# Fifth tile of x squared and scaled behind the first low parts; the gates' upper rows of the first tokens multiplied once for both halves

## The chip, the cores and the metric

The kernel runs on one core of one Trainium2 chip. The metric is the device time of one execution in microseconds (us); a measurement is the median of some executions.

## The reference

One layer of a hybrid block on x of 1024 tokens by 1024 channels, all float32: an RMS norm of x, one wide projection, an mLSTM branch and a dilated-attention branch, their gated sum, an output projection and a second RMS norm. What the change touches is the norm at the entry and the eight gate columns `if_pre`:

```python
h = rmsnorm(x, pre_w)
proj = h @ w_in
... if_pre ... = jnp.split(proj, idx, axis=-1)     # 2 * M_HEADS = 8 columns
gates = if_pre + b_if
i_pre = gates[..., :M_HEADS]
log_f = jax.nn.log_sigmoid(gates[..., M_HEADS:])
```

## The kernel before

**Splitting.** Every matrix product is made from float32 parts: a high part (a copy rounded to float32r, made by ScalarE) and a low part (the original less the high part, made by VectorE or GpSimd). A product is then three matmuls a k tile: high by high, low by high, high by low.

**Seven products a pair.** h, transposed, has 1024 channels by 1024 tokens and is cut in quadrants: B11 (upper channels, first tokens), B21 (lower channels, first tokens), T1 (upper channels, second tokens, less B11), B22 (lower channels, second tokens), and three more sums T2, T3, T4. Two columns of weight tiles (a "pair") are multiplied by it with seven products of 12 matmuls (P1 to P7) in place of eight. `seq` lists the products of all pairs; the first nine are P1, P2, P6, P5 of pair 0, P1 of pair 1, P7 of pair 0, P2 of pair 1, P4 and P3 of pair 0, and the tenth is P6 of pair 1. P1 reads B11, P2 reads B21, P6 reads T2, P5 reads T1, P7 reads T3, P4 reads T4, P3 reads B22. Each needs the high and the low part of its weights: for the products 0 to 3 the low part is made by GpSimd (`low`, L1077), for 4, 6, 7, 5 and 8 by VectorE or GpSimd by a table (`low_dve`, L375).

**The entry.** Eight tiles of 128 tokens of x arrive (`x_in`). Tiles 0 to 4 are squared and summed on ScalarE (`square`, L1504), get epsilon added on VectorE (`mean_square`, L2039), the reciprocal root on GpSimd (`reciprocal_root`, L1087), and are scaled on VectorE (`scale`, L2074). Tiles 5 to 7 are squared on VectorE (`late_square`, L2033) and scaled by a diagonal matrix that GpSimd makes (`diagonal`, L1094). TensorE transposes tiles 0 to 3 into eight banks (L1373). From each bank ScalarE makes the high part (`first_high`, L1510), VectorE the low part (`first_low`, L2043), and ScalarE a plain copy b_sb that frees the bank (`first_copy`, L1515). Product 0 waits for the first such copy. Behind product 1 TensorE transposes tiles 4 to 7 (`second_half`, L1380), from which ScalarE and VectorE make B22, T1, T2, and from those T3 and T4 with their high and low parts. All engines take their work in the order in which it is written; for the first nine products that order is written out by hand.

**The gates.** `iw` holds the gate columns' high and low parts side by side, so that a gate product of a k tile is two matmuls (high and low part of h). `gate_tokens` (L1249) multiplies for the first 512 tokens (half 0) B11 and B21, 16 matmuls, ahead of product 2, and for the second 512 tokens (half 1) B11, T1 and B22, 24 matmuls, ahead of product 8: B11 + T1 is the upper channels' part there. ScalarE copies both results into `gate_row` (L1583), SyncE sends it through DRAM into `gates4`, and VectorE reads it (`rows`, L1836).

The written orders that the change edits are, on ScalarE, L1529 to L1563; on VectorE, L2078 to L2083; on GpSimd, L1103 to L1107.

Of the kernel before, what the change touches and what calls it, by code (L numbers as in the profile page):

```python
# [13 lines left out]
P = 128  # L14
# [131 lines left out]
def hybrid_kernel(nc, x, w_in, w_if, w_pm, w_pa, w_out, b_gate, conv_wt, conv_bt, pre_wt, m_wt, post_w,  # L146
# [197 lines left out]
    for s in range(NSTEP):  # L344
        for it in items[s]:
            what = it[0]
            if what == "if":
                fill(("if", it[1]), "act")
# [50 lines left out]
    with ctx:  # L399
# [182 lines left out]
        x2_in = [sem(f"x2_in{i}") for i in range(4)]  # L582
# [7 lines left out]
        pe_y = sem("pe_y")  # L590

        x_sq = sem("x_sq")
# [6 lines left out]
        ring_act = sem("ring_act")  # L599
        keep_act = sem("keep_act")  # L600
# [8 lines left out]
        ysq_done, mg_hi = sem("ysq_done"), sem("mg_hi")  # L609

        v_step = sem("v_step")
        x_ms, x_sq_late, x_scaled = sem("x_ms"), sem("x_sq_late"), sem("x_scaled")
# [13 lines left out]
        m_ms, m_fac = sem("m_ms"), sem("m_fac")  # L626
# [3 lines left out]
        y_ms, y_read, y_done = sem("y_ms"), sem("y_read"), sem("y_done")  # L630

        g_ready = sem("g_ready")
        x_rs, x_norm = sem("x_rs"), sem("x_norm")
        s12_done = sem("s12_done")
        lo_pool = sem("lo_pool")
        m_rs, y_rs = sem("m_rs"), sem("y_rs")
# [136 lines left out]
        def _(sp):  # L773
# [95 lines left out]
            def piece(it):  # L869
# [9 lines left out]
                elif what == "if_out":  # L879
                    ring_taken(sp, ("if", 1))  # L880
# [152 lines left out]
            def x_again(t):  # L1033
                if t < 4:
                    sp.wait_ge(mg_done, 13 + t)
                else:
                    sp.wait_ge(y_done, t - 3)
                sp.dma_start(gst[t % 4][:], x[t * P:(t + 1) * P, :]).then_inc(x2_in[t % 4], 16)
# [19 lines left out]
        def _(g):  # L1058
# [28 lines left out]
            def reciprocal_root(t):  # L1087
                if t < 5:
                    g.wait_ge(x_ms, t + 1)
                else:  # L1090
                    g.wait_ge(x_sq_late, t - 4)
                TT(ssq[:, NT + t:NT + t + 1], ssq[:, t:t + 1], halfneg[:, 0:1], ALU.pow).then_inc(x_rs, 1)

            def diagonal(t):  # L1094
                reciprocal_root(t)
                g.wait_ge(x_rs, t + 1)
# [23 lines left out]
            for k in range(NSTEP):  # L1120
# [5 lines left out]
                for it in pool_late[k]:  # L1126
                    what = it[0]
                    if what == "norm":
                        h = it[1]
                        g.wait_ge(m_ms, h + 1)  # L1130
                        TT(mrs[:], msq[:, h % 2], halfneg[:], ALU.pow).then_inc(m_rs, 1)
            for t in range(NT):
                g.wait_ge(y_ms, t + 1)
                TT(yrs[:, t:t + 1], ysum[:, t:t + 1], halfneg[:, 0:1], ALU.pow).then_inc(y_rs, 1)
# [3 lines left out]
        def _(pe):  # L1138
# [110 lines left out]
            def gate_tokens(half):  # L1249
                b = work(("if", half))  # L1250
                if half == 0:
                    pe.wait_ge(iw_lo_done, 1)
# [1058 lines left out]
```

## Time and profile before

| | us |
|---|---|
| median of 3 runs | 1369.98 (1368.76 to 1371.14) |
| the profiled execution | 1369.94 |
| its span in the trace | 1368.1 |
| TensorE busy with matmuls | 1352.3 (99%) |
| VectorE, ScalarE, GpSimd busy | 794.5, 641.7, 569.2 |
| share of the chain that ended last on TensorE | 91% |

The span runs from the first to the last instruction; 1.8 us of the execution's time lie around it. Busy shares are means over the whole span: the entry is one stage and the rest another, and they are read apart by stretches. A matmul's duration in the trace is longer than the distance to the next, since matmuls overlap: 128x512 ones last about 390 ns and follow each other every 228 ns.

### The profile page before, as it was taken

What the parts mean: (1) busy time and instruction counts of PE and PEld (TensorE: products, weight loads), DVE (VectorE), ACT (ScalarE), POOL (GpSimd) and SP (SyncE); (2) the same over time, 40 slices, a digit from 0 to 9 for tenths busy, and PEclk for the clock granted to TensorE, in tenths of its full rate; (3) what the DMA queues carried; (4) which work ended last, traced back from release to release, by engine and by line L of the source; (5) the groups of instructions that cost most, each with busy time, mean ns of one, the idle gap of its engine ahead of it and who ended that gap; (6) DMA issues with size and microseconds to landing.
All of it is one profiled execution on the core that took longest, in us unless ns stands there. A gap on an engine that the chain in (4) does not pass through costs nothing.

```text
span 1368.1 us, 18779 instructions
## 1 busy us (share of the span) xinstructions
PE 1352.3 (99%) x6470; PEld 1127.3 (82%) x6470; DVE 794.5 (58%) x1260; ACT 641.7 (47%) x1320; POOL 569.2 (42%) x400
## 2 busy tenths in 40 slices
PE   7999999999999999999999999999999999999998
PEld 5788888888888888888888888888888888888786
DVE  5874438346543835877756575755644442997632
ACT  6644543543444455345445445544544553533421
POOL 5253435335443534654434445344333544454000
PEclk9999999999999999999999999999999999999999
DMA  6132233324233323455442634345343354966421
GB/s 194 51 76 65 69 74 90 96 48 126 76 85 72 84 79 61 149 173 144 114 145 66 188 104 134 100 127 175 87 150 97 93 188 165 345 200 196 183 97 58
DMA packets 210462, 165.02 MB, mean 121 GB/s; under 512 B 32400, under 2 KB 186544, under 8 KB 210368
## 3 DMA queue, kind: packets, MB, share of 16 engines
q1 hardware_dynamic: 210224, 163.75, 40.5%
q8 instruction: 53, 0.87, 0.3%
q14 instruction: 41, 0.34, 0.1%
q10 hardware_dynamic: 144, 0.07, 0.0%
HBM read 117.41 MB, written 40.08 MB: 115 GB/s over the span
## 4 chain that ended last, share of the span: by engine, by line
PE 91%; DVE 4%; issue 2%; ACT 1%; DMA 1%; SPq 1%; POOL 0%; DVEq 0%; POOLq 0%; ACTq 0%
PE proj L1244 69%; PE side L1189 3%; PE proj L1189 2%; PE side L1289 2%; PE side L1268 2%; PE side L1345 2%; PE side L1354 2%; PE proj L1170 2%; PE side L1170 2%; PE side L1277 1%; PE side L1317 1%; PE side L1350 1%; PE side L1300 1%; DMA x_sb<-x_in 1%; PE side L1362 1%
## 5 line engine op out<-in xcount | busy, mean ns | idle before, releaser
L1080 POOL TENSOR_TENSOR w_lo<-raw,w_hi 128x512 fp32r<-128x512 f32 x161 | 234.5, 1458 | 413.8 <-ACT w_hi L1456 413.7
L1244 PE MATMUL proj<-hi_T,w_hi 128*128 128x512 f32 x832 | 338.1, 406 | 2.2 <-ACT snap L1474 1.6
L1244 PE MATMUL proj<-hi_T,w_lo 128*128 128x512 f32 x832 | 325.2, 391 | 0.0
L1244 PE MATMUL proj<-lo_T,w_hi 128*128 128x512 f32 x832 | 324.1, 390 | 0.0
L1244 PE MATMUL proj<-hi_B,w_hi 128*128 128x512 f32 x624 | 254.1, 407 | 5.6 <-ACT b_sb L1518 4.0
L1244 PE MATMUL proj<-hi_B,w_lo 128*128 128x512 f32 x624 | 244.2, 391 | 0.0
L1244 PE MATMUL proj<-lo_B,w_hi 128*128 128x512 f32 x624 | 243.6, 390 | 0.0
L1080 POOL TENSOR_TENSOR w_lo<-s_sb,w_hi 128x512 fp32r<-128x512 f32 x104 | 156.7, 1510 | 153.5 <-ACT w_hi L1456 153.4
L1244 PEld LDWEIGHTS proj<-hi_T,w_hi 128*128 128x128 f32 x832 | 156.4, 188 | 36.0 <-issue 3.5
L1244 PEld LDWEIGHTS proj<-hi_T,w_lo 128*128 128x128 f32 x832 | 156.1, 188 | 34.2
L1244 PEld LDWEIGHTS proj<-lo_T,w_hi 128*128 128x128 f32 x832 | 156.6, 188 | 30.4
L1456 ACT ACTIVATE w_hi<-raw 128x512 fp32r<-128x512 f32 x216 | 135.2, 627 | 70.5 <-PE proj L1244 57.6
L1244 PEld LDWEIGHTS proj<-hi_B,w_hi 128*128 128x128 f32 x624 | 117.7, 189 | 29.9 <-ACT b_sb L1518 4.2
L1244 PEld LDWEIGHTS proj<-hi_B,w_lo 128*128 128x128 f32 x624 | 117.4, 188 | 25.4
L1244 PEld LDWEIGHTS proj<-lo_B,w_hi 128*128 128x128 f32 x624 | 117.8, 189 | 22.8
L1074 POOL TENSOR_TENSOR s_sb<-s_sb,raw 128x512 f32<-128x512 f32 x52 | 82.9, 1594 | 91.3 <-DVE w_lo L1887 90.5
L1456 ACT ACTIVATE w_hi<-s_sb 128x512 fp32r<-128x512 f32 x156 | 97.7, 627 | 37.9 <-PE proj L1244 28.9
L1887 DVE TENSOR_TENSOR w_lo<-s_sb,w_hi 128x512 fp32r<-128x512 f32 x52 | 43.9, 845 | 85.5 <-ACT w_hi L1456 85.5
L1068 POOL TENSOR_TENSOR s_sb<-raw 128x512 f32<-128x512 f32 x52 | 75.5, 1453 | 21.5 <-DVE w_lo L1887 21.4
L2001 DVE SCALAR_TENSOR_TENSOR tmp<-stage,cw,tmp 128x1023 f32<-128x1023 f32 (+2 forms) x48 | 76.1, 1585 | 0.7
L2144 DVE CUSTOM_DVE_ANT_0 prob<-side,mask_sb 128x128 f32<-128x128 f32 (+1 forms) x96 | 29.2, 347 | 67.3 <-PE side L1268 67.2
L1474 ACT ACTIVATE snap<-proj 128x512 f32<-128x512 f32 x52 | 31.1, 597 | 78.0 <-PE proj L1244 77.9
(253 smaller groups left out, 2014.5 us busy)
## 6 DMA issues: line engine op xcount, KB each, us to landing
raw<-w_in SPq DMA_DIRECT2D x95, 512.0 KB, 6.0
m_spill<-stage SPq DMA_DIRECT2D x16, 1024.0 KB, 5.6
chunk<-m_spill SPq DMA_DIRECT2D x32, 512.0 KB, 3.8
gate_spill<-stage SPq DMA_DIRECT2D x8, 1024.0 KB, 4.3
gst<-gate_spill SPq DMA_DIRECT2D x32, 256.0 KB, 3.2
share<-share_spill SPq DMA_DIRECT2D x12, 512.0 KB, 5.0
x_sb<-x_in SPq DMA_DIRECT2D x8, 512.0 KB, 7.6
hm_spill<-stage SPq DMA_DIRECT2D x4, 1024.0 KB, 8.8
```

What stands on the lines that cost most here:

```text
L1068: ins = TT(s1_sb[:], a21, a22, ALU.add)
L1074: ins = TT(s2_sb[:], s1_sb[:], a11, ALU.subtract)
L1080: TT(w_lo_ring[k % RING][:], src, w_hi_ring[k % RING][:].bitcast(F32), ALU.subtract).then_inc(lo_pool, 1)
L1170: mm = pe.matmul(pa_slot(t)[:, tokens], w[:, kt, :], m[:, kt, tokens], start=(kt == 0 and w is wh and m is at_hi), stop=(kt == AH - 1 and ...
L1189: mm = pe.matmul(y_slot(t)[:, columns], a[:, kt, :], w[i][:, j, columns], start=(kt == 0 and a is hi_part and w is out_hi), stop=(kt == KT ...
L1244: mm = pe.matmul(acc(p, which), w[:, kt, :], m[:, kt, :], start=(first and kt == 0 and w is wh and m is h_hi[b]), stop=(kt == 3 and w is w ...
L1268: mm = pe.matmul(b[:, at_ * P:(at_ + m) * P], qo_sb[(NG * h + g) % 4][:, n * P:(n + 1) * P], k_sb[g][:, (n + 1 - m) * P:(n + 1) * P], star ...
L1456: A(w_hi_ring[k % RING][:], src, ACT.Copy).then_inc(hi_done, 1)
L1474: A(snap[0][:], a, ACT.Copy).then_inc(u3_done, 1)
L1887: TT(w_lo_ring[k % RING][:], operand(p, weight_name(k)), w_hi_ring[k % RING][:].bitcast(F32), ALU.subtract).then_inc(lo_dve, 1)
L2001: ins = STT(t_[:, d:], src[:, 0:S - d], cw[:, t, 3 - d:4 - d], t_[:, d:], ALU.mult, ALU.add)
L2144: ins = V.tensor_tensor_reduce(out=prob_part(h, i)[:, part], in0=b[:, part], in1=mask, scale=-ASCALE, scalar=3.0e38, op0=ALU.add, op1=ALU. ...
```

## The change

1. **Order of the fifth tile.** On ScalarE `square(4)` moves from behind `high(0)` to behind `first_high(1)`. On VectorE `mean_square(4)` and `scale(4)` leave the loop ahead of the first low parts: `mean_square(4)` comes behind `first_low(2)`, `scale(4)` behind `late_square(5)`. On GpSimd `reciprocal_root(4)` comes behind `low(0)` in place of ahead of it.
2. **Gates.** A new step `if_top` ahead of product 2 multiplies B11 alone (8 matmuls) into the bank. ScalarE copies that partial sum into the second half of `gate_row`, between the high part T2,3 and the high part T1,0. The B21 part of half 0 (8 matmuls) moves to ahead of product 4, accumulates onto the same bank, and waits for that copy. Half 1 is then T1 and B22 alone, 16 matmuls, and VectorE adds its result to the stored part in place of ScalarE's copy. SyncE's `if_out` waits for both halves.
3. **Semaphores.** Several are merged with offsets (`row_sq`, `mean_sq`, `root`, `x_in` for the second reading of x); no instruction is added or moved by it.

```diff
-    items[2].append(("if", 0))
+    items[2].append(("if_top",))
+    items[4].append(("if", 0))
     items[8].append(("if", 1))
-    act_late[2].append(("if", 0))
-    act_late[8].append(("if", 1))
+    act_late[4].append(("if", 0))
+    dve_late[9].append(("if", 1))
...
                 elif what == "if_out":
+                    ring_taken(sp, ("if", 0))
                     ring_taken(sp, ("if", 1))
...
             for t in range(4):
                 reciprocal_root(t)
+            low(0)
             reciprocal_root(4)
-            low(0)
             low(1)
...
+            def gate_top_rows():
+                copied(pe, 2)
+                pe.wait_ge(iw_lo_done, 1)
+                gate_tokens(bank[0], [(kt, "B11") for kt in range(4)], True, False).then_inc(pe_gate, 1)
+
+            def gate_half(half):
+                b = work(("if", half))
+                if half == 0:
+                    pe.wait_ge(gate_top, 1)
+                    mm = gate_tokens(b, [(kt, "B21") for kt in range(4, 8)], False, True)
+                else:
+                    mm = gate_tokens(b, [(kt, name) for name, o in (("T1", 0), ("B22", 4)) for kt in range(o, o + 4)],
+                                     True, True)
                 mm.then_inc(pe_ring, 1)
...
             high(0)
-            square(4)
             act.wait_ge(start_in, 16 * NSTART)
             first_high(0)
             first_high(1)
+            square(4)
             first_copy(0)
...
             h_high("T2", 3, 8)
+            act.wait_ge(pe_gate, 1)
+            A(gate_row[:, half_of(1)], bank[0], ACT.Copy).then_inc(gate_top, 1)
             for j in range(4):
                 h_high("T1", j, 2 * j + 1)
...
+                elif what == "if":
+                    dve.wait_ge(pe_ring, ring_no["if", 1] + 1)
+                    dve.wait_ge(gate_top, 1)
+                    TT(gate_row[:, half_of(1)], bank[ring_no["if", 1] % BANKS], gate_row[:, half_of(1)], ALU.add
+                       ).then_inc(ring_dve, 1)
...
-            for t in range(5):
+            for t in range(4):
                 mean_square(t)
                 scale(t)
-            for kt in range(4):
+            for kt in range(3):
                 first_low(kt)
+            mean_square(4)
+            first_low(3)
             late_square(5)
+            scale(4)
             first_low(4)
```

## Rows read from the trace of the kernel before

**Rows 1.** Stretches: us, busy (count) of PE, PEld, DVE, ACT, POOL; clock; DMA.

```profile
17.20:20.00 2.80, 2.77 (x7) 2.19 (x8) 2.21 (x3) 2.80 (x6) 0.00 (x0) 0.50 1.20 290
20.00:26.60 6.60, 4.97 (x19) 3.10 (x18) 5.70 (x10) 5.10 (x10) 6.28 (x6) 0.99 0.22 50
36.80:55.00 18.20, 17.70 (x74) 13.06 (x73) 17.82 (x30) 12.74 (x24) 0.00 (x0) 1.00 0.07 18
63.50:1368.10 1304.60, 1296.52 (x6211) 1085.13 (x6209) 748.06 (x1188) 600.59 (x1248) 544.84 (x372) 1.00 0.41 120
```

**Rows 2.** TensorE's waits over the whole run: total us, times, longest.

```profile
PE proj L1244 <- ACT b_sb L1518: 4.0, 1, 4.0
PE proj L1244 <- DVE lo_B L2046: 1.6, 2, 0.8
```

**Rows 3.** Chain that ended last, in order of time: start us, us, what.

```profile
36.90 2.18 ACT hi_T L1526 x4
...
43.83 0.69 DVE lo_T L2071
...
55.12 5.47 PE side L1259 x24
```

**Rows 4.** Timeline of ScalarE: start us, us, engine, line, operation, [idle before].

```profile
10.57 0.63 ACT L1456 ACTIVATE w_hi<-raw 128x512 fp32r<-128x512 f32 x1 [0.64 <-DMA raw<-w_in]
12.05 1.06 ACT L1508 ACTIVATE tmp<-x_sb 128x1024 f32<-128x1024 f32 x1 [0.85 <-DMA x_sb<-x_in]
...
13.11 1.25 ACT L1513 ACTIVATE hi_B<-proj,prew 128x512 fp32r<-128x512 f32 x2
16.49 0.69 ACT L1518 ACTIVATE b_sb<-proj,prew 128x512 f32<-128x512 f32 x1 [2.13 <-DVE lo_B L2046]
...
55.28 0.58 ACT L1583 ACTIVATE gate_row<-side 128x512 f32<-128x512 f32 x1
```

**Rows 5.** Timeline of VectorE, 11 to 23 us.

```profile
11.35 0.75 DVE L2076 TENSOR_SCALAR x_sb<-x_sb,ssq 128x1024 f32<-128x1024 f32 x1 [0.66 <-POOL ssq L1092]
...
14.05 1.74 DVE L2076 TENSOR_SCALAR x_sb<-x_sb,ssq 128x1024 f32<-128x1024 f32 x1 [0.66 <-POOL ssq L1092]
...
19.11 1.22 DVE L2036 CUSTOM_DVE_ANT_0 x_junk<-x_sb 128x1024 f32<-128x1024 f32 x1
...
20.92 1.65 DVE L2036 CUSTOM_DVE_ANT_0 x_junk<-x_sb 128x1024 f32<-128x1024 f32 x1
```

**Rows 6.** Timeline of GpSimd, 10 to 22 us.

```profile
10.77 0.55 POOL L1092 TENSOR_TENSOR ssq<-ssq,halfneg 128x1 f32<-128x1 f32 x1 [0.93 <-DVE ssq L2041]
...
13.99 1.26 POOL L1080 TENSOR_TENSOR w_lo<-raw,w_hi 128x512 fp32r<-128x512 f32 x1
20.08 1.41 POOL L1080 TENSOR_TENSOR w_lo<-raw,w_hi 128x512 fp32r<-128x512 f32 x1 [4.84 <-ACT w_hi L1456]
```

**Rows 7.** Timeline of TensorE, 17 to 64 us.

```profile
17.23 0.80 PE L1244 MATMUL proj<-hi_B,w_hi 128*128 128x512 f32 x1 [3.98 <-ACT b_sb L1518]
...
26.60 0.27 PE L1394 MATMUL proj<-ident,x_sb 128*128 128x128 f32 x1
...
63.51 0.48 PE L1244 MATMUL proj<-hi_T,w_hi 128*128 128x512 f32 x1
```

**Rows 8.** Timeline of VectorE, 57 us.

```profile
57.03 0.69 DVE L1887 TENSOR_TENSOR w_lo<-s_sb,w_hi 128x512 fp32r<-128x512 f32 x1
```

**Rows 9.** Timeline of GpSimd, 57 to 64 us.

```profile
57.86 1.30 POOL L1068 TENSOR_TENSOR s_sb<-raw 128x512 f32<-128x512 f32 x1 [21.37 <-DVE w_lo L1887]
...
61.34 2.54 POOL L1080 TENSOR_TENSOR w_lo<-s_sb,w_hi 128x512 fp32r<-128x512 f32 x2 [0.74 <-ACT w_hi L1456]
```

**Rows 10.** Timeline of SyncE's DMA issues, 66 us.

```profile
66.86 0.35 SPq L885 DMA_DIRECT2D gates<-if_spill  x1
```

**Rows 11.** DMA issues, 60 to 76 us: count, KB each, us to landing.

```profile
gates<-if_spill SPq DMA_DIRECT2D x1, 64.0 KB, 1.9
```

**Rows 12.** Timeline of VectorE, 75 us.

```profile
75.44 0.19 DVE L1841 TENSOR_REDUCE m_rows<-ident 32x8 f32<-32x32 f32 x1
```

More of the change, by code:

```diff
@@ L599, in hybrid_kernel @@
         ring_act = sem("ring_act")
+        gate_top = sem("gate_top")
         keep_act = sem("keep_act")
@@ L1247, in product, with gate_tokens @@
                 mm.then_inc(pe_prod, 1)
[L1249 to L1252, printed above, removed]
-                    parts = [(kt, name) for name, o in (("B11", 0), ("B21", 4)) for kt in range(o, o + 4)]
-                else:
-                    parts = [(kt, name) for name, o in (("B11", 0), ("T1", 0), ("B22", 4)) for kt in range(o, o + 4)]
+            def gate_tokens(b, parts, first, last):
                 for i, (kt, name) in enumerate(parts):
@@ L1258, in gate_tokens @@
                     for m in (h_hi[name], h_lo[name]):
-                        mm = pe.matmul(b[:], iw[:, kt, :], m[:, kt % 4, :], start=(i == 0 and m is h_hi[name]),
-                                       stop=(i == len(parts) - 1 and m is h_lo[name]))
+                        mm = pe.matmul(b, iw[:, kt, :], m[:, kt % 4, :], start=(first and i == 0 and m is h_hi[name]),
+                                       stop=(last and i == len(parts) - 1 and m is h_lo[name]), skip_group_check=True)
+                return mm
+            def gate_top_rows():
[10 more added lines that the diff above has]
+                                     True, True)
                 mm.then_inc(pe_ring, 1)
@@ L1401, in _ @@
                     what = it[0]
-                    if what == "if":
-                        gate_tokens(it[1])
+                    if what == "if_top":
+                        gate_top_rows()
+                    elif what == "if":
+                        gate_half(it[1])
                     elif what == "cols":
@@ L1580, in piece @@
                 if what == "if":
-                    half = it[1]
-                    act.wait_ge(pe_ring, ring_no["if", half] + 1)
-                    A(gate_row[:, half * HALF:(half + 1) * HALF], bank[ring_no["if", half] % BANKS][:], ACT.Copy
-                      ).then_inc(ring_act, 1)
+                    act.wait_ge(pe_ring, ring_no["if", 0] + 1)
+                    A(gate_row[:, half_of(0)], bank[ring_no["if", 0] % BANKS], ACT.Copy).then_inc(ring_act, 1)
                 elif what == "log":
@@ L2020, in piece @@
                         dve.wait_ge(sq_done, NT * (h + 1))
-                        TS(msq[:, h % 2], msq[:, h % 2], 1.0 / MD, 4.0 * EPS, ALU.mult, ALU.add).then_inc(m_ms, 1)
+                        TS(msq[:, h % 2], msq[:, h % 2], 1.0 / MD, 4.0 * EPS, ALU.mult, ALU.add).then_inc(mean_sq, 1)
                     else:
-                        dve.wait_ge(m_rs, h + 1)
+                        dve.wait_ge(root, ROOT_M + h + 1)
                         TT(mfac[:], mrs[:], rden[:, h % 2], ALU.mult).then_inc(m_fac, 1)
+                elif what == "if":
+                    dve.wait_ge(pe_ring, ring_no["if", 1] + 1)
+                    dve.wait_ge(gate_top, 1)
+                    TT(gate_row[:, half_of(1)], bank[ring_no["if", 1] % BANKS], gate_row[:, half_of(1)], ALU.add
+                       ).then_inc(ring_dve, 1)
                 elif what == "small":
@@ L2231, in result @@
                     columns = half_of(half)
-                    dve.wait_ge(ysq_done, 2 * t + half + 1)
+                    dve.wait_ge(row_sq, SQ_Y + 2 * t + half + 1)
                     if half:
-                        STT(ysum[:, t:t + 1], ysq[:, t, 0:1], EPS, ysq[:, t, 1:2], ALU.add, ALU.add).then_inc(y_ms, 1)
+                        STT(ysum[:, t:t + 1], ysq[:, t, 0:1], EPS, ysq[:, t, 1:2], ALU.add, ALU.add).then_inc(mean_sq, 1)
                     elif t == 0:
@@ L2241, in result @@
                 dve.wait_ge(y_read, 2 * t + 2)
-                dve.wait_ge(y_rs, t + 1)
-                dve.wait_ge(x2_in[t % 4], 16 * (t // 4 + 1))
+                dve.wait_ge(root, ROOT_Y + t + 1)
+                dve.wait_ge(x_in[t], 32)
                 parts = [slice(0, DM)] if t < NT - 1 else [half_of(0), half_of(1)]
```

48 lines of the change are left out of this document (24 added, 24 removed).

## The prediction

> **What bounds the kernel now.** I read the stretches first [rows 1]. From 63.5 us to the end TensorE is busy for 1296.5 of 1304.6 us, at full clock. Whatever the change gains or loses must happen ahead of that point, and then it moves the end one for one, because nothing behind 63.5 us has slack to take it up or to give. The change edits only steps ahead of 66 us. In that part TensorE has idle time, and the list of its waits says for whom: 4.0 us once for the first plain copy b_sb, 1.6 us in two pieces for low parts of B21 [rows 2]. Then I read the chain that ended last [rows 3]: between 36.9 and 43.8 us it does not run on TensorE but through ScalarE's high parts into VectorE's low parts, and VectorE is busy 17.82 of 18.20 us from 36.8 to 55 us [rows 1]. So the entry is a chain of VectorE and ScalarE, with TensorE bound by itself only between 26.6 us and some 30 us and from 55 us on. The question for every part of the change is therefore: does it sit on that chain, and which engine is late at 63.5 us, when product 9 (P6 of pair 1) starts [rows 7]?
>
> **Part 1: eight gate matmuls less.** Half 1 had 24 gate matmuls in 5.47 us [rows 3], 0.228 us each; 16 are left, so 8 x 0.228 = 1.82 us of TensorE's time go. Half 0 keeps its 16, but 8 of them move from ahead of product 2 to ahead of product 4, where TensorE would otherwise wait: the chain of high and low parts sets when the products 2 to 7 can run, so this move neither costs nor gains (the cover is VectorE's 17.82 of 18.20 us [rows 1]; were it gone, the eight would still be the same eight). The 1.82 us lie at 58.6 to 60.4 us, in a stretch bound by TensorE. How much is kept depends on what is late next. Product 9 needs its weights' low part, and that comes along another chain: VectorE's low part of product 8 starts at 57.03 us and takes 0.69 us [rows 8]; it frees the buffer for GpSimd's first sum of pair 1, which starts at 57.86 us, and behind the second sum and ScalarE's high part GpSimd makes two low parts from 61.34 us in 2.54 us [rows 9], so the first is there at 61.34 + 1.27 = 62.61 us. Product 9 started at 63.51 us [rows 7]. It can come forward to about 62.65 us and no further while that chain stays where it is: **0.85 us of the 1.82 are kept, 0.97 are lost in a new wait** for GpSimd's low part.
>
> **Part 2: the added copy on ScalarE.** The copy of the partial gate sum is a 128x512 copy like the existing gate_row copy, 0.58 us [rows 4]; back to back such operations follow each other at less than their duration (four high parts in 2.18 us [rows 3], 0.54 each), so I take 0.5 us. It stands ahead of the high part T1,0, which is where the chain runs at 36.90 us [rows 3]. Its own input is early: the 8 matmuls behind the transposes end about 2 us before. Queued behind it on ScalarE are T1's and B22's high parts, two weight high parts, one snapshot and the first high part of T3, for which VectorE's low part at 43.83 us waits [rows 3]. There is no gap on ScalarE between, so that low part starts 0.5 us later, and with it VectorE's whole row of work to 57.03 us [rows 8] and the chain of part 1. **Cost 0.5 us on the chain** (0.3 if small gaps of VectorE take up some, 0.6 if the full duration counts). Half 1's copy, taken off ScalarE at 62.7 us, gains nothing there. Its substitute, an add on VectorE of about 0.7 us (as the low part in [rows 8]), comes behind VectorE's work at 65.6 us, where VectorE has nothing for some 5 us: nothing. It makes the gates ready for SyncE some 3 us later. Their way back was issued at 66.86 us [rows 10] and landed 1.9 us after its issue [rows 11]; VectorE reads them at 75.44 us [rows 12]. 66.86 + 3.1 + 0.35 + 1.9 = 72.2 us, 3 us early: nothing. SyncE's next queued issues, pair 3's weights, wait anyway for low parts of pair 1 at 71 us.
>
> **Part 3: the fifth tile moved.** In before, ScalarE squares tile 4 at 12.05 us, the first high part starts at 13.11 us and the first plain copy, for which product 0 waits, at 16.49 us [rows 4]; that copy waited for VectorE's first low part, which stood behind scale(4), from 14.05 us for 1.74 us [rows 5]. Taking scale(4) out of the way looks like 1.5 us. Two things take it back. **First, a collision.** The same scaling of tile 3 took 0.75 us [rows 5]; the scaling of tile 4 took 1.74 because GpSimd's low(0) had begun 0.06 us earlier, at 13.99 us for 1.26 us [rows 6]. The new order on GpSimd puts low(0) directly behind the root of tile 3, which starts at 10.77 us and takes 0.55 [rows 6], to 11.3 us; low(0)'s input, ScalarE's high(0), runs from 10.57 us for 0.63 us [rows 4] and is ready at 11.2 us. So low(0) starts at about 11.29 us, 0.06 us ahead of scale(3) at 11.35 us [rows 5]: the very pattern of tile 4 now falls on tile 3, which holds up the last transposes by 1.74 - 0.75 = 0.99 us. The first high part comes at about 13.45 us, the second at 14.0, the square of tile 4 at 14.6 to 15.7, the first copy at 15.7 in place of 16.49 us: product 0 starts 0.8 us earlier than 17.23 us [rows 7]. **Second, the work is only deferred.** scale(4) (0.75 us) and its epsilon (0.15 us) now lie between the low parts for which product 1 waits one by one. VectorE's row up to there gains 0.8 us and takes 0.9 us more. And scale(4) comes due as late_square(5) ends (1.22 us long [rows 5]), at which point GpSimd's low(1), held up by it, is due too, as at 20.08 us when it took 1.41 us [rows 6]. If low(1) goes first, scale(4) waits some 1.2 us, against which late_square(6), which took 1.65 us [rows 5] with low(1) beside it, gets 0.45 us shorter and a second wait of GpSimd's falls away; my walk through the three engines gives the low parts of B21 0.6 us late. If scale(4) goes first they are on time. I take the middle: **the transposes of the second tokens, at 26.60 us [rows 7], start 0.3 us later (0.0 to 0.6)**, and the chain behind them moves with them.
>
> The port is where a rule of the Trainium skill bears on this. It says ("SBUF — State Buffer", section "Who interferes with whom") that VectorE in a two-port mode and GpSimd share one pair of ports, that whoever issues first holds it for a whole instruction and that the other is fully blocked. The rows of tiles 3 and 4 above agree: 0.75 us alone, 1.74 us begun 0.06 us behind GpSimd. By that rule the order of two starts 0.06 us apart decides a whole microsecond, which is the rival "no collision" below.
>
> **The sum.** Front +0.3, copy +0.5, matmuls -0.85: -0.05 us. The span was 1368.1 us and 1.84 us lie around it, 1369.94 us for the profiled execution, 0.04 us from the median. 1369.94 - 0.05 = 1369.9 us.
>
> **The rivals.**
> - *No collision at tile 3.* If the first weights land only 0.1 us later, high(0) ends behind 11.35 us and scale(3) goes first. The last transposes then stay in place, product 0 starts about 1.7 us earlier, and with the deferred 0.9 us and the second collision the transposes at 26.60 us start 0.3 us earlier, 0.9 us if scale(4) also wins. -0.6 + 0.5 - 0.85 = -0.95: 1369.0 us. For it: margins of 0.06 us against the landing of a DMA. Against it: the profiled execution's own times.
> - *The cap is not there.* If the low part of product 9 is made early enough after all, or the copy finds a gap, all 1.82 us are kept: +0.3 + 0.5 - 1.82 = -1.0 us, or without a collision -1.9: 1368.0 to 1368.9 us. Against it stands the order GpSimd, ScalarE, GpSimd between 57.86 and 61.34 us [rows 9], which nothing in the change touches.
> - *Slower: TensorE's clock falls in product 1.* The granted clock was 0.50 (1.2 GHz) from 17.2 to 20 us, behind 3.98 us of idle time [rows 7], and 0.99 from 20 to 26.6 us [rows 1], with two idle pieces of 1.6 us together [rows 2]. The change starts product 0 earlier and product 1 no earlier, so TensorE's idle pieces before each k tile of B21 grow to 1.1 to 1.2 us. If the clock falls to the lower level there, the transposes from 26.60 us, 6.4 us of work bound by TensorE, run at half speed for, say, the 2.8 us of the low stretch of [rows 1]: +1.4 us, 1371.3 us; for all 6.4 us and a little of the gate matmuls, +3.2 to +6: 1373 to 1376 us. It decides as soon as the idle pieces ahead of the transposes bring the clock down, which those of 0.8 us did not and that of 3.98 us did.
> - *The gates come late.* Were the way through DRAM more than 3 us slower than I think, VectorE would stand still at 75 us and hold low parts: +0.5 to +1 us, 1370.7 us.
> - *The order does not matter at all* (the b_sb wait is taken by another input, such as the channel weights): the front term is +0.9 to 1.0, 1370.5 us; the change then does not do what its first part says.
>
> **How the numbers follow.** Forecast 0.45, no collision 0.25, no cap 0.1, clock 0.08 (half of it over 2.74 us), late gates 0.05, no effect of order 0.07. A difference of 0.2%, 2.74 us, is about what a measurement of this kernel can tell from no change. Only the high end of the clock case passes it upward: slower 0.04. Downward it takes no collision, no cap and both small races won (-2.8 us): faster 0.04. The rest, 0.92, is within. The cases without the clock lie between 1368.0 and 1370.9 us; the runs of before scatter by 1.2 us around their median, so a median of few moves by half of that: 1367.7 to 1371.4 us.
>
> **What would show it.** In the profile of after: scale(3) at 1.74 us with low(0) just ahead of it (or 0.75 us, the rival); the first b_sb copy at about 15.7 us; the first transpose of the second tokens at 26.9 us; the gate copy between two high parts near 37 us with no gap, and T3's first low part near 44.6 us; 16 gate matmuls ahead of product 8; a wait of some 0.9 us of TensorE ahead of product 9 or of pair 0's transposes of v, ended by GpSimd or ScalarE; product 9 at 63.5 us within 0.5. The prediction is wrong if product 9 starts by more than 1 us off that, if VectorE has gaps ahead of T3's low parts that take the copy up, or if the time behind product 9 is not 1304.6 us within its scatter.

## The result, and the profile after

| | before | after |
|---|---|---|
| median, us (20 runs each) | 1370.68 (1368.76 to 1372.31) | 1372.16 (1370.30 to 1375.04) |
| ratio after / before | | 1.0014 (95%: 1.0007 to 1.0020) |
| the profiled execution, us | 1369.94 | 1372.18 |
| its span | 1368.1 | 1370.4 |
| first transpose of the second tokens | 26.60 | 27.95 |
| product 9 starts | 63.51 | 64.25 |
| product 10 starts | 66.71 | 68.34 |
| product 10 to the end of the span | 1301.4 | 1302.0 |

The change costs 1 to 2.7 us. That is within 0.2% of before, as the largest of the chances had it, but 0.8 us above the upper end of the range. The stretches of after come first; the columns are those of [rows 1].

```profile
17.20:20.00 2.80, 2.80 (x9) 2.12 (x8) 2.80 (x6) 2.80 (x6) 1.20 (x2) 0.50 1.19 290
20.00:26.60 6.60, 4.52 (x12) 2.63 (x11) 6.27 (x9) 3.92 (x7) 6.30 (x7) 0.76 0.20 48
36.80:55.00 18.20, 17.03 (x73) 12.89 (x72) 17.41 (x29) 13.25 (x24) 0.78 (x1) 1.00 0.01 2
63.50:1370.40 1306.90, 1297.28 (x6212) 1085.39 (x6212) 747.81 (x1189) 601.49 (x1250) 547.13 (x373) 1.00 0.41 120
```

The granted clock from 20 to 26.6 us is 0.76 of full speed, where it was 0.99 [rows 1], and 12 matmuls ran there where 19 did. TensorE's waits of after (total us, times, longest):

```profile
PE proj L1251 <- ACT b_sb L1536: 2.3, 1, 2.3
PE proj L1251 <- DVE lo_B L2069: 2.1, 3, 1.1
...
PE side L1316 <- issue: 0.9, 1, 0.9
...
PE proj L1251 <- DVE k L1837: 0.6, 1, 0.6
```

The wait for b_sb is down from 4.0 to 2.3 us, that for low parts of B21 is up from 1.6 to 2.1 in three pieces [rows 2]. The last two rows are new. One, ahead of the transposes of v (L1316) and so of product 9, is the cap that the prediction had. The view names no releaser for it ("issue"); the copy vr_sb that these transposes read, made by ScalarE behind the two high parts that wait for GpSimd's second sum, ends 0.10 us ahead of them (63.18 + 0.58 = 63.76 us), and GpSimd's low part for product 9 ends at 64.1 us. The other, for VectorE's sum k (L1837) ahead of product 10, is not in the prediction at all.

VectorE and GpSimd at tiles 3 and 4, timeline (start us, us, engine, line, operation, [idle before <- what ended it]):

```profile
11.31 1.77 DVE L2099 TENSOR_SCALAR x_sb<-x_sb,ssq 128x1024 f32<-128x1024 f32 x1 [0.66 <-POOL ssq L1099]
...
19.58 1.76 DVE L2099 TENSOR_SCALAR x_sb<-x_sb,ssq 128x1024 f32<-128x1024 f32 x1
```

```profile
11.27 1.27 POOL L1087 TENSOR_TENSOR w_lo<-raw,w_hi 128x512 fp32r<-128x512 f32 x1
...
19.36 1.44 POOL L1087 TENSOR_TENSOR w_lo<-raw,w_hi 128x512 fp32r<-128x512 f32 x1 [0.86 <-ACT w_hi L1474]
```

GpSimd's low(0) begins 0.04 us ahead of scale(3), which takes 1.77 us where it took 0.75 [rows 5]; low(1) begins 0.22 us ahead of scale(4), which takes 1.76. TensorE in product 1 and up to the second tokens, and ScalarE with the added copy:

```profile
16.50 0.50 PE L1251 MATMUL proj<-hi_B,w_hi 128*128 128x512 f32 x1 [2.27 <-ACT b_sb L1536]
...
23.86 0.71 PE L1251 MATMUL proj<-hi_B,w_hi 128*128 128x512 f32 x1 [0.78 <-DVE lo_B L2069]
24.37 0.63 PE L1251 MATMUL proj<-lo_B,w_hi 128*128 128x512 f32 x1
24.80 0.63 PE L1251 MATMUL proj<-hi_B,w_lo 128*128 128x512 f32 x1
...
27.95 0.27 PE L1410 MATMUL proj<-ident,x_sb 128*128 128x128 f32 x1
```

```profile
15.76 0.69 ACT L1536 ACTIVATE b_sb<-proj,prew 128x512 f32<-128x512 f32 x1
...
37.99 0.58 ACT L1580 ACTIVATE gate_row<-side 128x512 f32<-128x512 f32 x1
38.47 1.66 ACT L1544 ACTIVATE hi_T<-sum_T 128x512 fp32r<-128x512 f32 x3
```

The matmuls from 24.37 us follow each other every 0.43 us: the lower of TensorE's two levels (1.2 GHz), for a second time. And this is the meeting that the prediction missed: two operations of VectorE and GpSimd that want the shared port at the same time. VectorE's and then GpSimd's timeline, with TensorE behind them:

```profile
64.14 1.76 DVE L1899 TENSOR_TENSOR s_sb<-raw,s_sb 128x512 f32<-128x512 f32 x1 [1.50 <-POOL w_lo L1087]
65.82 1.77 DVE L1905 TENSOR_TENSOR w_lo<-raw,w_hi 128x512 fp32r<-128x512 f32 x1
67.52 0.68 DVE L1837 TENSOR_TENSOR k<-snap,proj 128x512 f32<-128x512 f32 x1
68.11 0.68 DVE L2046 TENSOR_TENSOR gate_row<-side,gate_row 128x512 f32<-128x512 f32 x1
```

```profile
62.84 2.51 POOL L1087 TENSOR_TENSOR w_lo<-s_sb,w_hi 128x512 fp32r<-128x512 f32 x2 [0.74 <-ACT w_hi L1474]
65.72 1.32 POOL L1087 TENSOR_TENSOR w_lo<-raw,w_hi 128x512 fp32r<-128x512 f32 x1 [0.37 <-ACT w_hi L1474]
```

```profile
63.86 0.63 PE L1316 MATMUL side<-ident,vr_sb 128*128 128x128 f32 x4 [0.85 <-issue]
64.25 0.47 PE L1251 MATMUL proj<-hi_T,w_hi 128*128 128x512 f32 x1
...
68.34 0.47 PE L1251 MATMUL proj<-hi_T,w_hi 128*128 128x512 f32 x1 [0.64 <-DVE k L1837]
```

VectorE's low part of product 11, at 65.82 us, takes 1.77 us, because GpSimd's low part of product 12 began 0.10 us ahead of it. In before the same two came in the other order:

```profile
64.35 0.68 DVE L1887 TENSOR_TENSOR w_lo<-raw,w_hi 128x512 fp32r<-128x512 f32 x1
...
64.99 1.29 POOL L1080 TENSOR_TENSOR w_lo<-raw,w_hi 128x512 fp32r<-128x512 f32 x1 [1.12 <-ACT w_hi L1456]
```

k stands behind that low part on VectorE, so it comes 1.1 us later, and product 10 waits for it. The chain that ended last of after, in order of time, runs past product 9 through these very operations:

```profile
62.84 1.28 POOL w_lo L1087
...
64.14 0.21 DVE s_sb L1899
...
65.82 1.77 DVE w_lo L1905
67.59 0.61 DVE k L1837
...
68.34 3.68 PE proj L1251 x15
```

### The profile page after: what moved, and what is told of

It reads as the page before. It is cut to its first block, busy times and chain, and to the rows that moved or that the text cites. A ratio compares the mean times of both kernels' runs of the same rounds, so it can differ in the third digit from the quotient of the medians.

```text
span 1370.4 us, 18767 instructions
## 1 busy us (share of the span) xinstructions
PE 1352.3 (99%) x6462; PEld 1126.7 (82%) x6462; DVE 793.0 (58%) x1261; ACT 641.6 (47%) x1320; POOL 570.1 (42%) x400
## 4 chain that ended last, share of the span: by engine, by line
PE 86%; DVE 4%; issue 2%; DMA 2%; SPq 1%; ACT 0%; POOL 0%; DVEq 0%; POOLq 0%; ACTq 0%
PE proj L1251 65%; PE side L1196 3%; PE proj L1196 2%; PE side L1305 2%; PE side L1284 2%; PE side L1361 2%; PE side L1370 2%; PE proj L1177 2%; PE side L1177 2%; PE side L1293 1%; PE side L1333 1%; PE side L1366 1%; SPq L914 1%; PE side L1316 1%; DMA share<-share_spill 1%
```

## The experiments

All milestones are from timelines, one profiled execution of each kernel, in us. "T2" is the first transpose of the second tokens, and "copy's stretch" the distance from T2's first low part to T3's first low part (both on VectorE), in which the added copy lies. "T3 to product 9" starts at T3's first low part. It is the cleanest measure of what an edit behind the copy does: T2 to T2's first low part takes about 9.4 us in some kernels and about 9.65 in others (9.54 in e10, 10.74 in e3) for reasons that lie ahead of the gates' half, and "T2 to product 9" carries that difference with it.

| kernel | T2 | copy's stretch | T2 to product 9 | T3 to product 9 | product 9 to 10 | VectorE low part of product 11 | product 10 |
|---|---|---|---|---|---|---|---|
| before | 26.60 | 7.59 | 36.91 | 19.68 | 3.20 | 0.68 | 66.71 |
| after | 27.95 | 7.99 | 36.30 | 18.92 | 4.09 | 1.77 | 68.34 |
| e1_order_alone | 27.46 | 7.59 | 36.62 | 19.65 | 3.21 | 0.68 | 67.29 |
| e2_gates_alone | 26.76 | 8.00 | 36.55 | 18.90 | 4.10 | 1.77 | 67.41 |
| e3_low0_behind | 28.18 | 7.99 | 37.64 | 18.91 | 4.10 | 1.77 | 69.92 |
| e5_gates_copy_in_gap | 27.84 | 7.59 | 36.87 | 19.63 | 4.09 | 1.77 | 68.80 |
| e8_low12_behind_low11 | 26.53 | 7.99 | 36.27 | 18.90 | 3.20 | 0.68 | 66.00 |
| e9_gates_low12_behind | 25.63 | 7.99 | 36.54 | 18.90 | 3.19 | 0.68 | 65.36 |
| e10_no_collision | 27.38 | 8.00 | 36.45 | 18.91 | 3.19 | 0.68 | 67.02 |
| e11_filled_gaps | 27.88 | 8.00 | 36.30 | 18.91 | 4.09 | 1.78 | 68.27 |
| e13_gates_low12_low8 | 27.41 | 8.00 | 36.02 | 18.63 | 3.19 | 0.68 | 66.62 |
| e14_copy_gap_low12 | 26.26 | 7.59 | 36.64 | 19.67 | 3.20 | 0.68 | 66.10 |
| e12_copy_gap_low8_low12 | 28.07 | 7.59 | 36.87 | 19.64 | 3.21 | 0.68 | 68.15 |
| e7_before_low8_first | 25.75 | 7.60 | 36.88 | 19.65 | 3.20 | 0.68 | 65.83 |

The front needs columns of its own, since two DMA landings move it. In the old order T2 hangs on the landing of the fifth tile of x: it comes 12.55 us behind the start of scale(4) in e9 (13.08 to 25.63 us) and in e12 (15.52 to 28.07 us), 2.4 us apart. So 26.60 us of before is one draw. In the six kernels with the new order, ScalarE squares the fifth tile at 14.1 to 15.0 us without a wait, so this landing did not set T2 in them; that of the start weights did in two (e3, e11):

| kernel | scale(3): start, us | to first b_sb | b_sb to T2 | both | clock 20 to 26.6 us |
|---|---|---|---|---|---|
| before (old order) | 11.35, 0.75 | 5.14 | 10.11 | 15.25 | 0.99 |
| after | 11.31, 1.77 | 4.45 | 12.19 | 16.64 | 0.76 |
| e1_order_alone | 11.62, 1.75 | 4.42 | 11.42 | 15.84 | 0.99 |
| e3_low0_behind | 11.20, 0.75 | 4.34 | 12.64 | 16.98 | 0.76 |
| e8_low12_behind_low11 | 11.69, 0.75 | 3.43 | 11.41 | 14.84 | 1.00 |
| e10_no_collision | 11.70, 0.75 | 3.43 | 12.25 | 15.68 | 0.57 |
| e11_filled_gaps | 11.33, 0.75 | 4.17 | 12.38 | 16.55 | 1.00 |

The intervals of the ratios below reach some 1.2 us to either side, so of 1 us and less the traces tell more than the medians.

### Each half of the change alone

e1 is the kernel before with the new order of the fifth tile, no gate edit:

```diff
+            low(0)
             reciprocal_root(4)
-            low(0)
...
             first_high(1)
+            square(4)
...
+            mean_square(4)
+            first_low(3)
             late_square(5)
+            scale(4)
```

> The kernel before with the fifth tile's new order alone; the gates stay as they were. Theory (the new order is the loss, through three costs on one chain: the scaling of tile 3 held up by GpSimd's low(0), the scaling of tile 4 by low(1), and TensorE's clock lower ahead of the second transposes): the first transpose of the second tokens starts about 27.9 us in place of 26.60, GpSimd's first sum of pair 1 about 1.1 us later than 57.86, and since nothing shortens TensorE's work the kernel is 1.1 to 2.0 us slower than before. Rival (the gates' new copy and the split are the loss, the order is even): within 0.3 us of before, product 9 at 63.5 us.

Measured: median 1371.21 us, ratio 1.0002 (0.9993 to 1.0011). scale(3) took 1.75 us beside low(0), and T2 came 15.84 us behind its start, 0.59 us more than in before. TensorE waited 1.12, 0.78 and 0.84 us ahead of three k tiles of product 1, and yet the clock stayed up:

```profile
20.00:26.60 6.60, 3.85 (x15) 2.22 (x13) 6.57 (x9) 3.90 (x7) 6.30 (x7) 0.99 0.22 48
```

So at T2 the order alone, with the collision and with the clock kept, is worth the upper end of what was forecast for it (0.6 us). Some of it comes back at once: in before GpSimd's last diagonal matrix was ready only at 27.26 us, behind T2 (26.60), and TensorE's first group of six transposes by it took 0.93 us from start to start of the next group; with the new order the matrix is ready ahead of T2 and the group takes 0.67 us. Counted from scale(3), T2's first low part is 0.33 us later than in before (25.22 and 24.89 us), and product 10 is 0.31 us later (55.67 and 55.36 us). In the time that is not told from nothing. The 1.1 us and more of the expectation were missed.

e2 is the opposite, the gates' half alone:

```diff
+            reciprocal_root(4)
             low(0)
-            reciprocal_root(4)
...
-            for t in range(4):
+            for t in range(5):
                 mean_square(t)
                 scale(t)
```

> The change without the fifth tile's new order: gates multiplied once, the copy of the partial sum ahead of T1's high parts. Theory (the order is the loss; the gates' part costs 0.4 us of chain for the copy and keeps 0.8 us of the 1.82): T3's first low part at 44.2 us, product 9 at 63.1 us, 0.4 us faster than before. Rival (the gates' part is the loss): slower than before by 0.5 us or more.

Measured: median 1371.33 us, ratio 1.0006 (0.9997 to 1.0015). Up to product 9 it went as expected: T3's first low part 0.40 us later against T2's, product 9 at 63.31 us, 36.55 us behind T2 in place of 36.91. These 0.36 us are +0.40 for the copy and -0.76 for the eight matmuls. But product 10 started 4.10 us behind product 9, not 3.20. VectorE's and GpSimd's timelines of e2:

```profile
64.89 1.77 DVE L1905 TENSOR_TENSOR w_lo<-raw,w_hi 128x512 fp32r<-128x512 f32 x1
66.59 0.67 DVE L1837 TENSOR_TENSOR k<-snap,proj 128x512 f32<-128x512 f32 x1
```

```profile
64.79 1.33 POOL L1087 TENSOR_TENSOR w_lo<-raw,w_hi 128x512 fp32r<-128x512 f32 x1 [0.37 <-ACT w_hi L1474]
```

The same meeting as in after, with the same margin of 0.10 us. It belongs to the gates' half: all five kernels that have that half and leave this order alone show it (after, e2, e3, e5, e11), with margins of 0.10 us, and e1 does not. From T2 to product 10 e2 needs 40.65 us and before 40.11: the gates' half, meant to save 1.8 us of matmuls, loses 0.5.

### The meeting at 65 us taken away

Theory from here on: the gate edit lets TensorE, and with it ScalarE, come forward against VectorE's chain. ScalarE no longer has the gate copy (62.68 us in before) and the transposes of v, whose copy it makes next, come earlier, so it hands product 12's high part to GpSimd before VectorE gets to product 11's low part. That these two causes bring ScalarE forward is read from the timelines; no run parts them. Rival: the wait for k is a matter of VectorE's lateness alone, and would be there without GpSimd. The edit holds GpSimd back by one operation; e8 is after with it, e9 is e2 with it:

```diff
+                    if k == 9:
+                        low_wait(g, 11)
                     low(k + LEAD)
```

> The changed kernel with one wait more: GpSimd's low part of product 12 waits until VectorE has made the low part of product 11. Theory (in the changed kernel these two meet, since TensorE and ScalarE come forward against VectorE; GpSimd wins by 0.1 us and VectorE's low part takes 1.77 us in place of 0.68, which holds up the sum that product 10 waits for): VectorE's low part of product 11 takes 0.7 us, TensorE's wait of 0.6 us ahead of product 10 goes, product 10 starts 3.2 us behind product 9 in place of 4.1, and the kernel is 0.9 us faster than the changed one. Rival (that wait only takes the place of one that comes anyway): product 10 moves by less than 0.3 us and the time stays.

> The gates' part alone with the same wait more, the fifth tile as in the kernel before. Theory: product 9 at 63.3 us and product 10 at 66.5 us, both 0.2 us ahead of the kernel before, which gives 0.2 us less than before; against the gates' part alone (product 10 at 67.4 us) 0.9 us less. Rival (the gates' part loses by something else): product 10 stays at 67.4 us or the gain is lost behind it.

Measured: e8 1370.75 us, 1.0001 (0.9993 to 1.0010); e9 1369.76 us, 0.9994 (0.9986 to 1.0003), where the change itself stands at 1.0014. VectorE and GpSimd in e9:

```profile
63.75 0.68 DVE L1907 TENSOR_TENSOR w_lo<-raw,w_hi 128x512 fp32r<-128x512 f32 x1
64.35 0.68 DVE L1839 TENSOR_TENSOR k<-snap,proj 128x512 f32<-128x512 f32 x1
```

```profile
64.50 1.29 POOL L1087 TENSOR_TENSOR w_lo<-raw,w_hi 128x512 fp32r<-128x512 f32 x1 [1.23 <-DVE w_lo L1907]
```

The low part takes 0.68 us again, in both kernels, and product 10 follows product 9 by 3.20 and 3.19 us. T2 to product 10 is 39.73 us in e9, against 40.65 in e2 and 40.11 in before. That is the 0.9 us of the missed step, and the rival is out. By the medians the step is only suggested: the interval of e8 touches that of after. With the meeting gone the gates' half does what was forecast for it: 0.38 us earlier than before. In e8 low(0) also happened to come at 11.79 us, 0.10 us behind scale(3), which took 0.75 us while low(0) took 1.78 us. From scale(3) to T2 it needed 14.84 us, 1.00 less than e1 with the collision and the same clock, and 0.41 less than before: the rival "no collision at tile 3", which had 0.3.

### The collisions at the front taken away

e3 is after with low(0) held behind scale(3):

```diff
+            g.wait_ge(x_scaled, 4)
             low(0)
```

> The changed kernel with one wait more: GpSimd's low(0) waits until tile 3 is scaled. Theory (the first collision is real but mostly hidden: product 1 waits for low parts that stand behind late squares and the deferred scaling, not for product 0): scaling of tile 3 takes 0.75 us in place of 1.77, the last transposes start at 12.1 us, the first copy b_sb at 14.8 us, the low parts of B21 come 0.3 to 0.9 us earlier, and the kernel gains 0.3 to 1.2 us on the changed one. Rival (the collision has no share in the loss): no difference from the changed kernel, 1.5 us over before.

Measured: 1372.32 us, 1.0012 (1.0004 to 1.0021), no better than after. scale(3) took 0.75 us, but two things ate the microsecond. ScalarE's first high part, timeline of e3, now waited for the start weights:

```profile
13.34 1.26 ACT L1532 ACTIVATE hi_B<-proj,prew 128x512 fp32r<-128x512 f32 x2 [1.16 <-DMA ifw<-w_if]
```

so b_sb came 4.34 us behind scale(3), not 3.43 as in e8. And the clock was low again from product 1's later k tiles on and into the transposes behind T2: 12.64 us from b_sb to T2, and T2's first low part 10.74 us behind T2 instead of 9.39. The expectation was missed by a landing and by the clock, not by the port of tile 3. (The collision of scale(4) with low(1) was still there, 1.77 us.) e10 holds both low(0) and low(1) behind their scalings, and has the edit of e8:

```diff
+            g.wait_ge(x_scaled, 4)
             low(0)
             reciprocal_root(4)
+            g.wait_ge(x_scaled, 5)
             low(1)
```

> The changed kernel with three waits more on GpSimd: low(0) behind the scaling of tile 3, low(1) behind that of tile 4, the low part of product 12 behind that of product 11. Theory (three meetings on the shared ports plus the low clock are the loss): both scalings and the low part take 0.75, 0.75 and 0.68 us, the low parts of B21 come 1.0 us earlier than in the changed kernel, product 10 starts at 66.3 to 66.8 us, and the kernel is 1.5 to 2.2 us faster than the changed one, no slower than before. Rival (the new order is worse by itself): product 10 behind 67.5 us.

Measured: 1370.03 us, 0.9995 (0.9986 to 1.0003), 2.1 us less than after by the medians. Both scalings took 0.75 us; late_square(6) now met low(1), 1.85 us in place of 1.21, and TensorE waited 2.2 us for that low part. The last low part of B21 came at 24.52 us, 1.0 us earlier than in after, as expected; product 10 came at 67.02 us, a little later than the 66.3 to 66.8 of the expectation. By the ratios to before, e10 (0.9995) and after (1.0014) are clear of each other. The clock, e3's windows row above e10's:

```profile
20.00:26.60 6.60, 4.16 (x12) 2.08 (x11) 6.06 (x9) 3.90 (x7) 6.30 (x8) 0.76 0.30 77
```

```profile
20.00:26.60 6.60, 5.21 (x11) 3.22 (x12) 5.26 (x8) 4.18 (x9) 6.30 (x7) 0.57 0.22 51
```

From b_sb to T2 the two kernels with the clock kept need 11.41 and 11.42 us (e8, e1), the three with the fallen clock 12.19 to 12.64 (after, e10, e3). So the collision at tile 3 is worth 1.0 us where no landing covers it (e1 against e8), and the fallen clock costs 0.8 us in after and in e3 1.2 us up to T2 and 1.35 us behind it (10.74 for 9.39). In e3 it stayed low until 31.0 us, in after until 27.4 us. e10 is another case: its clock was 1.00 up to 20.9 us, through all of product 0, fell in the wait of 2.2 us for low(1), and stayed low until 27.7 us, so its 0.84 us has more than one cause.

e11 fills TensorE's idle pieces in product 1 of after with small matmuls, whose results are overwritten:

```diff
+                        if name == "P2" and kt < 3:
+                            copied(pe, 3)
+                            for i in range((4, 6, 6)[kt]):
+                                pe.matmul(pb[2][:, 0:P], ident[:], ident[:], start=True, stop=True)
```

> The changed kernel with 16 matmuls of 128 columns more, which fill TensorE's idle pieces in product 1 (4, 6 and 6 ahead of its first three k tiles) and whose results are overwritten. Theory (the granted clock falls a second time because those pieces are long): the granted clock stays at its upper level from 20 to 27 us, the k tiles of product 1 take 0.7 us each in place of 1.3, the transposes of the second tokens start 0.7 us earlier than in the changed kernel, 27.2 us, and the kernel is 0.5 to 0.7 us faster than the changed one. Rival (the fall comes from something else): the clock falls there all the same and the time stays.

Measured: 1371.71 us, 1.0009 (1.0000 to 1.0017). The clock was 1.00 from 20 to 26.6 us, but each six of the small matmuls took 1.26 us, more than the pieces that they were to fill, and T2 came at 27.88 us. Since e8's clock also stayed up with the pieces unfilled, the run says nothing on what keeps it.

### The copy in another place

e5 is e2 with the copy between T3's second and third high parts, where ScalarE waits for sums, and the B21 matmuls ahead of product 5 instead of 4:

```diff
-    items[4].append(("if", 0))
+    items[5].append(("if", 0))
...
             for j in range(2):
                 h_high("T3", j, 9 + j)
+            act.wait_ge(pe_gate, 1)
+            A(gate_row[:, half_of(1)], bank[0], ACT.Copy).then_inc(gate_top, 1)
             for j in range(2, 4):
```

> The gates' part alone in another order: the copy of the partial sum stands between T3's second and third high part, where ScalarE had a gap of 0.76 us, and the B21 half is multiplied ahead of pair 0's P7. The fifth tile is as in the kernel before. Theory (the copy costs by where it stands): T3's first low part stays at 43.8 us, product 9 comes at 62.7 us, 0.8 us faster than before and 0.4 us faster than the gates' part with the copy ahead of T1. Rival (the copy's place is free): the same as the gates' part alone.

Measured: 1372.46 us, 1.0009 (1.0000 to 1.0018). T3's row is 7.59 us, as in before: the copy's 0.40 us are gone. But T2 to product 9 is 36.87 us, 0.32 more than in e2, so 0.7 us are lost behind T3. ScalarE and VectorE in e5:

```profile
51.05 0.60 ACT L1492 ACTIVATE snap<-proj 128x512 f32<-128x512 f32 x1 [2.28 <-PE proj L1251]
```

```profile
52.20 0.69 DVE L2096 TENSOR_TENSOR lo_T<-sum_T,hi_T 128x512 fp32r<-128x512 f32 x1 [0.82 <-ACT hi_T L1544]
```

The eight matmuls, moved to ahead of product 5, put that product and its snapshot back. ScalarE stands still 2.28 us for it (1.42 in e2), with T4's high parts queued behind, and VectorE 0.82 us, where it had no such gap in e2. From T3's first low part to product 9 e5 needs 19.63 us, as before does, where e2 needs 18.90. So the place ahead of product 4 was free and the next one is not. e14 is e5 with the edit of e8:

> The gates' part with the copy of the partial sum between T3's second and third high part, the B21 half ahead of P7 of pair 0, and the low part of product 12 behind that of product 11. Theory (the copy costs 0.4 us by its place): from VectorE's first low part of T2 to its first of T3 7.6 us as in the kernel before, in place of 8.0; 0.4 us faster than the same with the copy ahead of T1 (e9). Rival: no difference.

Measured: 1370.44 us, 1.0004 (0.9995 to 1.0013). T2 to product 9 is 36.64 us against 36.54 in e9: no gain over leaving the copy on the chain. The 0.40 us of the copy are gained (7.59 for 7.99) and 0.77 us lost behind it (19.67 for 18.90).

### The cap ahead of product 9

GpSimd's first sum waits for VectorE's low part of product 8 [rows 8, 9]. That low part was moved ahead of B22's last two low parts:

```diff
-            for j in range(4):
+            for j in range(2):
                 h_low("B22", j, 8 + j + 1, h_ready["B22"])
...
+            for j in range(2, 4):
+                h_low("B22", j, 8 + j + 1, h_ready["B22"])
```

e13 is e9 with it, e7 is before with it, and e12 is e5 with it and the edit of e8.

> The gates' part alone, low part of product 12 behind that of product 11, and VectorE's low part of product 8 two places earlier (behind the second of B22's four low parts in place of the fourth). Theory (the prediction's cap: of the 1.82 us one microsecond is lost because product 9 waits for GpSimd, whose chain starts at that low part): GpSimd's first sum of pair 1 comes 1.2 us earlier against the first copy b_sb, product 9 comes 1.0 us earlier against it, the kernel is about 1 us faster than the same one without this edit (e9). Rival (the cap is VectorE's own row, or ScalarE's snapshot): product 9 moves by less than 0.4 us.

> The kernel before with one edit: the low part of product 8 two places earlier. Theory (in the kernel before TensorE itself is the bound between its 24 gate matmuls and product 9, so GpSimd's chain has 0.9 us of slack there): GpSimd's first sum 1.2 us earlier, product 9 where it was, time within 0.2 us. Rival (the chain was the bound already before): faster by 0.5 us or more.

> All three edits: copy in the gap, low part of product 8 two places earlier, low part of product 12 behind that of product 11; the fifth tile as in the kernel before. Theory: the 1.82 us of the eight matmuls are kept whole, about 1.8 us (0.13%) faster than the kernel before, the fastest of all. Rival (a new meeting of GpSimd and VectorE or another wait ahead of product 10 takes the gain back): less than 0.8 us.

Measured: e13 1370.42 us, 0.9997 (0.9988 to 1.0006); e7 1370.22 us, 0.9999 (0.9990 to 1.0008); e12 1370.74 us, 0.9999 (0.9990 to 1.0008). In e7 the cap is not what binds: T2 to product 9 is 36.88 us against 36.91, as it should be where TensorE itself is late. In e13 it is 36.02 us against 36.54 in e9, but 0.25 of these 0.52 us lie between T2 and T2's first low part (9.39 and 9.65 us), far ahead of the edit. From T3's first low part to product 9 it is 18.63 against 18.90 us: 0.27 us gained where 1.0 was expected, and so the case of the rival (less than 0.4). GpSimd's timeline of e13:

```profile
57.64 2.21 POOL L1075 TENSOR_TENSOR s_sb<-raw 128x512 f32<-128x512 f32 x1 [20.58 <-DVE w_lo L1907]
```

Against T3's first low part the sum came 1.20 us earlier than in e9 (12.84 and 14.04 us), as expected, but took 2.21 us where it takes 1.30 [rows 9]: it now stands beside VectorE's last two low parts of B22, of which the first began ahead of it. The chain moved ahead ran into the same port from the other side. In e7 the sum took 1.60 us and VectorE's two low parts 2.38, where two take 1.29. e12 gained nothing of the copy's 0.4 us: 36.87 us to product 9, with VectorE's two low parts at 2.39 us. The expected 1.8 us did not come; the rival's case did.

## Why the prediction was wrong, by its steps

The sum of the profiled executions is closed: T2 +1.35, T2's first low part -0.25 against T2, copy +0.40, matmuls -0.76 (what is left of product 9's +0.74), product 9 to 10 +0.89, behind product 10 +0.61; together 2.24 us, the difference of the two executions. Against the forecast of -0.05 us the miss is 2.3 us: 0.9 at product 10, 0.8 at the front (1.10 for 0.3), 0.6 behind product 10, and the two other terms even out.

- **What bounds the kernel: right up to its last step.** Ahead of 63.5 us it is the chain through ScalarE and VectorE. But "nothing behind 63.5 us has slack", taken to mean that product 9 carries the result, was the step that failed. The change moves VectorE's low part of product 11 by +1.47 us and GpSimd's low part of product 12, which follows ScalarE and TensorE, by +0.73. The trace of before had the margin: the first began 0.64 us ahead of the second (64.35 and 64.99 us). A relative shift of 0.74 us turned that into 0.10 us behind. The working followed the chain to product 9 and stopped there; its sentence that the gate copy taken off ScalarE "gains nothing there" looked at the copy's own time and not at what ScalarE then hands on earlier. **+0.89 us, missed whole**; e2 shows it with the gates' half alone, e8 and e9 take it away.
- **Matmuls: right.** -0.85 us forecast of 1.82, -0.76 measured (19.68 to 18.92 us); the cap by GpSimd's chain is there, as a wait of 0.85 us ahead of the transposes of v. The rival without the cap is out; e13, by an edit of its own, won 0.27 us of it.
- **The copy: right.** +0.5 us forecast, +0.40 to 0.41 measured in all eight kernels with the copy ahead of T1's high parts, and 0 where the copy was moved (e5, e14, e12). VectorE had no gap to take it up.
- **The front: right in kind, mis-sized.** +0.3 us (0.0 to 0.6) forecast, +1.35 measured at T2 and +1.10 at T2's first low part, from where the chain goes on. VectorE's part, the last low part of B21 at 25.54 us in place of 24.97, is +0.57 at T2 and, with the 0.25 us that come back behind T2, +0.32 on the chain: e1, with 0.59 and then 0.33, shows the same, and that is the forecast. scale(3) at 1.77 us and b_sb at 15.76 us came as forecast to 0.1 us. The term that was left out is the clock: the other 0.78 us, from that low part to T2, are TensorE at 1.2 GHz again. That is the rival "clock falls in product 1", to which 0.08 was given and which the range did not take in. The clock was low within product 1 in 3 of the 5 kernels with the new order and no filling (after, e3, e10; not e1, e8), in one profiled execution of each. In the eight kernels with the old order, whose idle pieces ahead of B21's low parts are 0.75 to 1.0 us, it did not fall a second time, so "which those of 0.8 us did not" held.
- **No collision at tile 3**: it came in 2 of the 4 kernels that leave it to chance (e8, e11; not after, e1), so 0.25 was rather low for it. The forecast of 0.3 us earlier than before at T2 was near the 0.41 of e8. What no step had is that T2 of before itself is a draw that a landing moves by 2.4 us.
- **Late gates, and an order without effect**: neither. b_sb was 0.7 us earlier, and the add on VectorE at 68.11 us made nothing wait.
- **One for one behind product 9**: only within 1 us. Over 14 profiles the stretch from product 10 to the end lasted 1300.9 to 1303.0 us, with no pattern by edit; 0.61 us of the difference between the two profiles is of this kind. The predicted time started from an execution 0.7 us under the later median of before, too. The range, 1367.7 to 1371.4 us, is narrower than its own working (1368.0 to 1370.9 us with 0.6 us on either side gives 1367.4 to 1371.5); the measured median lies outside both.

What the runs settle by their medians is less than what the traces settle: after is slower than before; e9 and e10, measured beside before in another series, lie some 2 us under after, with intervals that do not touch its own; no kernel here is shown faster than before (e9 is the best, 0.9994, 0.9986 to 1.0003). What stays open is what decides whether the clock falls a second time.

## What to carry to other kernels

An edit that shifts two engines against each other has to be followed to every place where they use the shared port next, not to the first wait: list the pairs of VectorE and GpSimd operations whose starts, in the profile of before, are no further apart than the edit can shift them (here 0.64 us apart, shifted by 0.74), since each such order can cost 1 us. Where one such order is wanted, write it as a wait: one on GpSimd, which had slack, bought back 0.9 us in the traces. And work taken from a busy engine in a chain of three is kept only up to the next engine's chain, here 0.8 of 1.8 us.

## What the runs showed of the hardware

- **VectorE's operation that begins second takes 1.0 to 1.1 us longer, at margins of 0.04 to 0.23 us.** The scaling of a tile on VectorE takes 0.75 us alone, and 1.74 to 1.78 when GpSimd's low part began ahead of it. Plain VectorE sums with two inputs in SBUF do the same: 0.68 us alone, 1.76 to 1.78 beside it. That is a little less than what is left of GpSimd's operation of 1.26 to 1.33 us, which the full block of the prediction's rule would cost. The prediction had used this for the entry's operations (the scaling, late_square(6)) and not for the sums. The Trainium skill has both ("SBUF — State Buffer", section "Who interferes with whom": a VectorE instruction with two SBUF inputs contends with a GpSimd instruction that reads SBUF); the trace agrees, 1.77 against 0.68 us, and by that rule the missed step could have been looked for.
- **It works in both directions, and a sum with one input in PSUM was spared.** GpSimd's sum took 2.21 us beside VectorE's low parts (e13), 1.30 alone, and its low(0), begun 0.10 us behind scale(3), took 1.78 us (e8), 1.27 alone. VectorE's k, one of whose inputs (proj) lies in PSUM, ran from 64.35 us in e9 in its 0.68 us with GpSimd's low part beside it from 64.50, in 1.29, and from 64.95 us in before with GpSimd's from 64.99, in 0.68 and 1.29.
- **TensorE's clock fell a second time in some executions.** With idle pieces of 1.05 and 0.78 us ahead of k tiles of product 1, the granted clock from 20 to 26.6 us was 0.76 in after; with 1.12, 0.78 and 0.84 us it was 0.99 in e1, and with 1.15, 0.78 and 0.84 it was 1.00 in e8. The first fall is as open: of two kernels whose TensorE waited 2.9 us ahead of product 0, e9 had 0.65 from 17.2 to 20 us, and e7 1.00 there and from 20 to 26.6 us. The idle time before the fall does not tell them apart. The second fall cost 0.8 us in after, and 2.6 us in e3, where it lasted into the transposes.
